# A hybrid SSM / short-convolution / expert-retrieval layer: reordering the stages ahead of the first expert gather

## The reference

```
sh1, sc1, g1, sh2, sc2, g2 = split(silu(cond) @ w_mod + b_mod)      # one row for context, one for latent
h = rmsnorm(x, norm1_g) * (1 + sc1) + sh1
u, cb, cc, ch = split(h @ w_in)
y_ssm  = glu(gelu(S5 scan of u, forward + backward, 32 groups x 64 complex states, + d_skip * u))
y_conv = cb * conv3(cc * ch)                                        # width 3 along rows
x = x + g1 * (concat(rmsnorm(y_ssm), headwise rmsnorm(y_conv)) * out_norm_g) @ w_out
h = rmsnorm(x, norm2_g) * (1 + sc2) + sh2
x = x + g2 * peer(h)
y = rmsnorm(x, final_norm_g)
```

## Time and profile before

| | |
|---|---|
| median of 3 runs | 1988.73 us |
| lowest, highest | 1987.07, 1994.5 us |
| the profiled execution | 1987.85 us, its span 1986.1 us |
| PE busy | 1201.5 us, 60% |
| DVE busy | 1443.9 us, 73% |
| ACT busy | 375.6 us, 19% |
| POOL busy | 736.0 us, 37% |
| DMA | 745.90 MB, mean 376 GB/s |
| first gather issued | 234.18 us |

### The profile page before, as it was taken

The page is one execution under the profiler, slowest core; times in us unless marked ns, Lnnn a source line. Parts: engine busy times, 40 slices in busy tenths (PEclk is TensorE's granted clock), DMA queues, the critical chain, the costliest instruction groups (busy, mean ns, idle before and its releaser), DMA issues.

```text
span 1986.1 us, 22255 instructions
## 1 busy us (share of the span) xinstructions
PE 1201.5 (60%) x7540; PEld 465.5 (23%) x7540; DVE 1443.9 (73%) x3889; ACT 375.6 (19%) x845; POOL 736.0 (37%) x673
## 2 busy tenths in 40 slices
PE   5988988888867666666544443364344454444444
PEld 2557733333322222222111000021000011111001
DVE  8778367877766776766788777777777767877675
ACT  4241342122222221111111110121011111211110
POOL 3100132333433333343443444444444444344442
PEclk8999989999968877777655555575555556555555
DMA  8556499999989999999999999999999999999996
GB/s 337 170 186 209 155 394 383 358 394 389 395 339 390 382 393 394 401 403 388 421 421 420 415 417 413 421 407 414 416 415 420 409 414 410 416 421 404 415 414 258
DMA packets 126098, 745.90 MB, mean 376 GB/s; under 512 B 12112, under 2 KB 34896, under 8 KB 40352
## 3 DMA queue, kind: packets, MB, share of 16 engines
q0 software_dynamic: 92160, 671.13, 82.8%
q1 hardware_dynamic: 33824, 73.35, 10.5%
HBM read 741.78 MB, written 2.65 MB: 375 GB/s over the span
## 4 chain that ended last, share of the span: by engine, by line
DMA 31%; PE 29%; DVE 26%; issue 10%; ACT 2%; POOL 0%; DVEq 0%; POOLq 0%; SPq 0%; ACTq 0%
DMA r<-table,gidx 30%; DVE r L1675 8%; PE bank L843 7%; PE bank L811 6%; PE bank L920 3%; PE bank L931 2%; DMA r<-w_query 1%; DVE wgt L1687 1%; PE bank L778 1%; DVE r L1643 1%; DVE i L1617 1%; PE bank L539 1%; PE bank L638 1%; DVE i L1623 1%; DVE r L1618 1%
## 5 line engine op out<-in xcount | busy, mean ns | idle before, releaser
L1875 POOL DMA_INDIRECT r<-table,gidx x640 | 708.9, 1108 | 1063.9 <-PE bank L843 902.6
L1675 DVE CUSTOM_DVE_ANT_0 r<-r 128x1024 f32<-128x1024 f32 x640 | 779.9, 1224 | 310.9 <-DMA r<-table,gidx 292.3
L843 PE MATMUL bank<-r,wgt 128*32 128x512 f32 x2560 | 536.6, 923 | 727.7 <-DVE wgt L1687 709.0
L843 PEld LDWEIGHTS bank<-r,wgt 128*32 128x32 f32 x2560 | 61.4, 130 | 1102.7 <-DVE wgt L1687 1032.2
L1223 ACT ACTIVATE r<-r 128x2 f32<-128x2 f32 x320 | 65.1, 203 | 1045.7 <-DVE r L1675 1042.8
L811 PE MATMUL bank<-hT_r,r 128*128 128x512 f32 x256 | 120.4, 625 | 0.9 <-ACT hT_r L1079 0.9
L1684 DVE TENSOR_TENSOR r<-r 128x2 f32<-128x2 f32 x320 | 50.2, 157 | 82.0 <-ACT r L1223 82.0
L1687 DVE TENSOR_TENSOR wgt<-fold,r 128x64 f32<-128x64 f32 x320 | 72.0, 225 | 11.1
L811 PEld LDWEIGHTS bank<-hT_r,r 128*128 128x128 f32 x256 | 50.3, 202 | 75.9 <-issue 75.9
L1223 ACT ACT_TABLE_LOAD x51 | 65.4, 1283 | 0.9
L920 PE MATMUL bank<-hT_r,r 128*128 128x512 f32 x128 | 62.9, 636 | 0.0
(11 more groups left out here) (362 smaller groups left out, 1472.6 us busy)
## 6 DMA issues: line engine op xcount, KB each, us to landing
r<-w_mod SPq DMA_DIRECT2D x24, 1024.0 KB, 7.8
r<-w_query SPq DMA_DIRECT2D x15, 1024.0 KB
r<-table,gidx POOLq DMA_INDIRECT x640, 11.6
r<-w_tiles SPq DMA_DIRECT2D x12, 512.0 KB, 8.1
x_r<-w_tiles SPq DMA_DIRECT2D x10, 512.0 KB, 4.9
hT_r<-xT SPq DMA_DIRECT2D x4, 640.0 KB, 6.3
r<-w_u SPq DMA_DIRECT2D x1, 2048.0 KB, 31.3
r<-w_o SPq DMA_DIRECT2D x1, 2048.0 KB, 10.5
```

The lines of the kernel that those rows point to most:

```text
L843: last = mm(bank[ACC[b % 2][h]][to:to + TG, :], wgt[:, g % 2, e, :], rows[:, k % SLOTS, D + h * 512:D + (h + 1) * 512], start=(G % HEADS = ...
L1675: V.tensor_tensor_reduce(rows[:, s, 0:D], rows[:, s, 0:D], h2r[tg], 1.0, 0.0, ALU.mult, ALU.add, hid[:, par, k:k + 1]).then_inc(dot_done, 1)
L1875: G_.indirect_dma_start(rows[:, k % SLOTS, :], None, table, bass.IndirectOffsetOnAxis(gidx[:, e, k:k + 1], 0)).then_inc(row_in[k % SLOTS], 16)
```

## The change

Five regions are edited.

1. **`bc` is loaded in two parts**: its B half at its old place (`ld_bc`), its C half behind `w_u` (`ld_cc`).
2. **Front.** DVE makes input block 0 straight behind `Bb`, then the reciprocal, four scalings, the gains, four scalings. PE turns tiles 0, 1 behind slab 5 and 2, 3 behind slab 6, ahead of `mod_turn(0)`; ACT takes them ahead of the modulation. Tiles 4 to 7 are turned after k = 1; there is no group after k = 4.
3. **`CP`.** DVE makes all eight blocks; POOL's block, its buffer `tp` and `p9_ready` go, and POOL's `Bd` waits for `cp_ready`, of which there is now one.
4. **SP and slabs.** `WTC` begins with buffers 4 and 5; the glu's weights are loaded when two context tiles are through (`zc_mm` 2), ahead of tiles 6 and 7; `w_query` then goes ahead of tiles 8, 9, and `w_o` ahead of tiles 10, 11. Slab 20 is summed between the halves of M, 21 behind them, 22 ahead of `Y` instead of behind `conv_ctx(0)`. `spread_heads` stands ahead of output tile 6 instead of tile 4 (the order of tiles is 0, 1, 2, 3, 6, 7, 4, 5).
5. **DVE behind the scans.** Convolution and gate product come first (the gate product ahead of the last tap), segment 2 in place of 3, 3 in place of 4, and 4 behind the second normalised half. `lag_blocks` comes after the third step of the context scan.

```diff
-            sp.dma_start(bcs, bc).then_inc(ld_bc, 16)
+            sp.dma_start(bcs[:, 0:2], bc[:, 0:2]).then_inc(ld_bc, 16)
             for n in range(8):
                 load_mod(n)
             sp.dma_start(wu, w_u).then_inc(ld_wu, 16)
+            sp.dma_start(bcs[:, 2:4], bc[:, 2:4]).then_inc(ld_cc, 16)
...
-        WTC = [0, 1, 2, 3, 4, 5, 0, 1, 2, 3, 0, 1]
+        WTC = [4, 5, 0, 1, 2, 3, 0, 1, 2, 3, 0, 1]
...
-                    sp.wait_ge(zc_mm, (1, 2, 3, 4, 7, 8)[q - 6])
+                    sp.wait_ge(zc_mm, q - 3)
...
-            for q in range(4):
+            for q in range(2, 6):
                 load_conv_ctx(q)
             sp.wait_ge(us_mm, 2)
-            for q in range(4, 6):
+            for q in range(2):
                 load_conv_ctx(q)
             for n in range(18, 24):
                 load_mod(n)
-            for q in range(6, 10):
+            sp.wait_ge(zc_mm, 2)
+            for j in range(2):
+                sp.dma_start(wt[:, j, :, :], w_tiles[NCONV + j]).then_inc(wtg_in, 16)
+            for q in range(6, 8):
                 load_conv_ctx(q)
             sp.wait_ge(m_mm, 2)
             sp.dma_start(wqa, w_query[:, :, 0:DQ]).then_inc(ld_wq0, 16)
-            sp.wait_ge(zc_mm, 6)
-            for j in range(2):
-                sp.dma_start(wt[:, j, :, :], w_tiles[NCONV + j]).then_inc(wtg_in, 16)
-            for q in range(10, 12):
+            for q in range(8, 10):
                 load_conv_ctx(q)
             sp.wait_ge(mod_mm, 24)
             sp.dma_start(woA, w_o[:, 0:4, :, :]).then_inc(ld_woa, 16)
+            for q in range(10, 12):
+                load_conv_ctx(q)
...
+            pe.wait_ge(silu_done, 1)
+            for n in range(KD):
+                mod_slab(n)
+                if n in (5, 6):
+                    turn_input(2 * (n - 5))
+                    turn_input(2 * (n - 5) + 1)
+            mod_turn(0)
...
-                if k in (1, 4):
-                    for e in range(4):
-                        turn_input((0 if k == 1 else 4) + e)
+                if k == 1:
+                    for e in range(4, 8):
+                        turn_input(e)
...
                 last.then_inc(m_mm, 1)
-            mod_slab(20)
-            mod_slab(21)
+                mod_slab(20 + a)
+            mod_slab(22)
...
-            mod_slab(22)
             mod_slab(23)
...
-                    if first and m == 4:
+                    if first and m == 6:
                         spread_heads()
...
+            for e in range(4):
+                take_input(e)
             mod_rows(0)
             mod_take(0)
...
             dve.wait_ge(bb_ready, 1)
             chunk_inputs(0)
-            gains(1, COL_N1, 2)
+            dve.wait_ge(rms_act, 2)
+            link(V.reciprocal(rs, rs))
+            for k in range(KD):
+                if k == 4:
+                    gains(1, COL_N1, 2)
+                tt(hT[:, k, :], hT[:, k, :], rs, ALU.mult).then_inc(xs_ready, 1)
             for n in range(1, 4):
                 chunk_inputs(n)
...
-            for q4 in range(CP_POOL, NQ, 4):
+            dve.wait_ge(ld_cc, 16)
+            for q4 in range(0, NQ, 4):
...
-                if i == 4:
+                if i == 3:
                     lag_blocks()
...
-            link(*[stt(cvx[:, i, 0:CTX - 1], ccx[:, i, 1:CTX], cw[2][i], cvx[:, i, 0:CTX - 1], ALU.mult, ALU.add) for i in range(KS)])
-
             dve.wait_ge(sgc_ev, KS)
             tt(mixc[:, 0:KS, :], mixc[:, 0:KS, :], gTc, ALU.mult).then_inc(gluc_ev, 1)
-            segment_products(3)
+            link(*[stt(cvx[:, i, 0:CTX - 1], ccx[:, i, 1:CTX], cw[2][i], cvx[:, i, 0:CTX - 1], ALU.mult, ALU.add) for i in range(KS)])
+            segment_products(2)
...
             pool.wait_ge(bb_ready, 1)
-            pool.wait_ge(xs_ready, KD)
+            pool.wait_ge(cp_ready, 1)
             link(G_.memset(Bd, 0.0))
```

More of the change, by code:

```diff
@@ L114, in build @@
         P9r = part(r2, 10816, 576).rearrange("p (j r q) -> p j r q", j=Q + 1, r=2)
-        tp = part(r2, 11392, 576).rearrange("p (q j c) -> p q j c", q=4, j=Q + 1)
         tv = part(r2, 11968, 576)
@@ L251, in build @@
         cp_ready = sem("cp_ready")
-        p9_ready = sem("p9_ready")
+        ld_cc = sem("ld_cc")
         bb_ready = sem("bb_ready")
@@ L367, in build @@
         HID_AT = {3: (0,), 4: (1,), 5: (2,), 6: (3,), 7: ()}
-        CP_POOL = 4
         CW = MCH * P
@@ L514, in _ @@
                 mm(bank[5][:, 0:CTX], ones[:, :], sq[k % 2][:, 0:CTX], start=(k == 0), stop=(k == KD - 1)).then_inc(sq_used, 1)
[L515 to L518, removed]
             def turn_input(e):
@@ L600, in _ @@
             pe.wait_ge(bd_ready, 1)
-            pe.wait_ge(cp_ready, 2)
+            pe.wait_ge(cp_ready, 1)
             pe.wait_ge(dm_ready, 1)
@@ L1108, in _ @@
                 modulate(0, k, 1, CTX, T).then_inc(h_ready, 1)
-            for e in range(8):
+            for e in range(4, 8):
                 take_input(e)
@@ L1132, in _ @@
             last.then_inc(dm_ready, 1)
-            act.wait_ge(cp_ready, 2)
+            act.wait_ge(cp_ready, 1)
             act.wait_ge(bp_ready, 2)
@@ L1426, in _ @@
             V.tensor_copy(sv[:, 9, :], sv[:, 4, :]).then_inc(bb_ready, 1)
-            dve.wait_ge(rms_act, 2)
-            link(V.reciprocal(rs, rs))
-            for k in range(KD):
-                tt(hT[:, k, :], hT[:, k, :], rs, ALU.mult).then_inc(xs_ready, 1)
             def chunk_inputs(n):
@@ L1559, in _ @@
             link(*[stt(cvx[:, i, 1:CTX], ccx[:, i, 0:CTX - 1], cw[0][i], cvx[:, i, 1:CTX], ALU.mult, ALU.add) for i in range(KS)])
-            link(*[stt(cvx[:, i, 0:CTX - 1], ccx[:, i, 1:CTX], cw[2][i], cvx[:, i, 0:CTX - 1], ALU.mult, ALU.add) for i in range(KS)])
             dve.wait_ge(sgc_ev, KS)
             tt(mixc[:, 0:KS, :], mixc[:, 0:KS, :], gTc, ALU.mult).then_inc(gluc_ev, 1)
-            segment_products(3)
+            link(*[stt(cvx[:, i, 0:CTX - 1], ccx[:, i, 1:CTX], cw[2][i], cvx[:, i, 0:CTX - 1], ALU.mult, ALU.add) for i in range(KS)])
+            segment_products(2)
             dve.wait_ge(rms_c, 1)
             V.reciprocal(inv1[0], rt1[0]).then_inc(inv_ready, 1)
-            segment_add(3)
+            segment_add(2)
             dve.wait_ge(inv_mm, 1)
@@ L1572, in _ @@
             last.then_inc(mixc_ready, 1)
-            segment_store(3)
+            segment_store(2)
             dve.wait_ge(zc_mm, 12)
             tt(mixc[:, KS:KD, :].rearrange("p k t -> p (k t)"), cvx.rearrange("p k t -> p (k t)"), bank[2][:, :], ALU.mult).then_inc(cvx_ev, 1)
-            segment_products(4)
+            segment_products(3)
             dve.wait_ge(rms_c, 2)
             V.reciprocal(inv8, rt8).then_inc(inv_ready, 1)
-            segment_add(4)
-            segment_store(4)
-            V.tensor_copy(small[:, 2:3], eps_c[:, :]).then_inc(scan_lat, 1)
+            segment_add(3)
+            segment_store(3)
             dve.wait_ge(inv_mm, 2)
@@ L1587, in _ @@
             last.then_inc(mixc_ready, 1)
+            segment_products(4)
+            segment_add(4)
+            segment_store(4)
+            V.tensor_copy(small[:, 2:3], eps_c[:, :]).then_inc(scan_lat, 1)
             dve.wait_ge(ld_xc, 16)
@@ L1846, in _ @@
             pool.sem_inc(bd_ready, 1)
-            pool.wait_ge(p9_ready, 1)
-            pool.wait_ge(ld_bc, 16)
-            for q4 in range(0, CP_POOL, 4):
-                q = slice(q4, q4 + 4)
-                w = P9 if q4 < NPAIR else P9r
-                J = Q + 1
-                pw = [w[:, :, r, q].rearrange("p s (q a) -> p q s a", a=1).broadcast_to([P, 4, J, GC]) for r in range(2)]
-                cv = [bcs[:, 2 + r, q, :].rearrange("p q (a c) -> p q a c", a=1).broadcast_to([P, 4, J, GC]) for r in range(2)]
-                o = [CP[:, r, q, :, :] for r in range(2)]
-                T_ = G_.tensor_tensor
-                link(T_(o[0], pw[0], cv[0], ALU.mult), T_(tp, pw[1], cv[1], ALU.mult))
-                link(T_(o[0], o[0], tp, ALU.subtract))
-                link(T_(o[1], pw[0], cv[1], ALU.mult), T_(tp, pw[1], cv[0], ALU.mult))
-                link(T_(o[1], o[1], tp, ALU.add))
-                link(G_.tensor_scalar(o[1], o[1], -1.0, None, ALU.mult))
-            pool.sem_inc(cp_ready, 1)
             pool.wait_ge(mod_tr, 6)
```

4 lines of the change are left out of this document (removed).

## The result

The changed kernel takes **1972.91 us** (median of 5 runs, 1966.37 to 1977.83); the kernel before, run beside it on the same chip, took 1988.73 (5 runs, 1987.07 to 1994.5). The ratio is 0.9911, 95% interval [0.9886, 0.9936], which is 17.7 us less (the two medians themselves lie 15.8 apart). The forecast was 1972 in a range of 1965 to 1980. The time was right; the sum behind it was not right in every term, and the places where it failed are the useful part of what follows.

The account below looks back on a forecast made before the run. Expert gathers (DMA) set the pace from 900 us; before the first gather at 234 us the chain, mostly PE, counts. Terms 4.1+2.3+3.2+5.5+1.6 = 16.7 off 1987.85 give 1971.2; plus 0.88 for the median, 1972 us, range 1965 to 1980.

Parts of the forecast that it names:

- What bounds the kernel: Up to the first gather at 234 us, each microsecond saved on the chain comes off the end; everything behind slides.
- Input blocks ahead of the scalings: In the modulation, gains end at 38.7 and PE starts at 40.1: 4.1 us earlier, bounds 2.2 and 5.2.
- sign of being wrong: In the front: PE's turns waiting for DVE's blocks would show the prediction wrong.
- rival B: Modulation becomes late: turns at half clock hold slab 7, second stall appears; gain 10.3 us, time 1978.4; chance 0.12.
- Turned tiles: The u stage loses one of its two groups of four turns: 2.3 us.
- CP: PE's wait ahead of the third group of state products goes whole: 3.2 us, with 4.8 us of cover left.
- The issue stall: PE's 3.13 us stall before 151.93, read as instruction fetch queued behind two slabs: 1.6 us saved, 4.4 better to 3.1 worse.
- rival D: First u matmuls run warm (2.6 us) and the stall goes whole (4.4 for 1.6): gain 22.1, 1966.6 us; chance 0.15.
- Rival A: The stall before 151.93 has another cause, queues being taken in turn, and stays: gain 15.1, 1973.6 us; chance 0.15.
- SP's order and slabs: Earlier glu weights and moved slabs let the glu run at once, ending at 177.7 instead of 183.28: 5.5 us.
- DVE's order: Behind the scans, DVE would wait for PE's glu, not PE for DVE, so the new order gains nothing.
- `lag_blocks` earlier: On DVE, moves up one step: under 1 us, and PE waits for the scan's end anyway: 0.

Follow-up runs that it names:

- front_only: Kernel before with only input block 0 ahead of the scalings, turned tiles between the slabs and CP wholly on DVE: 1979.26 us, ratio 0.9950 to before.
- slabs_back: Changed kernel with slabs 20 and 21 behind M, 22 and 23 behind the first convolution pass, as before: 1972.68 us, ratio 0.9927 to before.
- sp_order_back: Changed kernel with SP's old order of loads and old buffers, glu weights behind six convolution tiles: 1973.76 us, ratio 0.9924 to before.
- dve_order_back: Changed kernel with DVE's old order behind the scans, such as segment 2 ahead of the convolution: 1978.88 us, ratio 0.9941 to before.

## Why the prediction was right, and where it was not

**What bounds the kernel: right.** Three comparisons of the whole change give 0.9911, 0.9897 and 0.9897, that is 17.7 to 20.5 us off the end, and the first gather starts 20.4 us earlier (mean of three profiles after, 213.2, against the mean of two before, 233.6). What is saved ahead of the first gather reaches the end, and the rest slides. It did not stay "unchanged within 3 us" in a pair of profiles, because single executions differ by up to 12 us there.

**Input blocks ahead of the scalings: right**, 4.7 for 4.1, inside its bounds. The sequence was as worked out (block 7.0, gains at 37.7, floor `w_u`). I had the clock come back midway, and the nine profiles of this front differ there. In seven PE summed slab 5 at full clock (1.07 us), and the `u` stage began at 39.2 to 40.0. In three of the seven (`front_only`, `slabs_back`, `sp_order_back`) the first turns then waited 0.93 to 1.05 us for DVE's block and took 1.82 to 1.97, at half clock, and full clock was back by the second turns. That wait was a sign of being wrong in the prediction; the start at 39.6 to 39.8 shows no loss from it. In the other two slab 5 took 1.93 and the start came at 41.0 and 41.3: rival B's mechanism, in two executions of nine, at 1.5 to 2 us. What ends PE's wait ahead of the first `u` matmul is `w_u` in four of the nine (39.2 to 40.0) and ACT's modulated tile in the other five, so both bind at about the same time. The first eight `u` matmuls took 6.17, mostly at half clock, as taken (5.37 to 6.36 over the nine).

**Turned tiles: right**, 2.3. **CP: the wait went and the cover was 4.7, as said, but the term was mis-sized:** 4.4 for 3.2. I counted the wait of 3.17 and overlooked that the row behind it already shows 96 state products in 5.45, which at full clock take 4.15. Here the half clock behind the wait went with the wait.

**The issue stall: mechanism half right, size wrong.** The step that failed is "I take half of the stall for half of the bytes". All of it went, 4.5 us with the half clock behind it, which is the upper bound that the prediction gave and rival D's value. The backlog explains 2.5 us of it; 2.0 stay without it, and there PE still goes on only 2.5 us behind the instruction packet. So the rows point to the fetch of instructions, as the prediction read it, but it is late for more than the backlog. The Trainium skill, DMA: Bandwidth & Descriptors, section Queues, rings and completion order, has each DMA engine take its queues in turn, packet by packet. The traces agree in so far as the packet came at 149.5, 1.5 us before the slab data ended; but with slabs in flight it came 3.3 to 4.2 us into `Y` instead of 1.4, so taking turns did not spare it a delay. Rival A, that the stall stays in the changed kernel, is refuted.

**SP's order and slabs: right in size**, 5.6 for 5.5 up to the end of the glu.

**DVE's order: wrong reading.** The failed step is "DVE then waits for PE's glu, not PE for DVE. Segment 2 no longer stands ahead of the convolution ... Nothing". I compared DVE's time on the old scale (free at 171.45) with a PE that had moved by 1 us (174.0). But the edits ahead moved PE by 15.7 us and the latent scan, which DVE starts when the context scan is through, by only 10.9. On the new scale PE's input is there at 158.4 and DVE free at 160.5; DVE is the later one, and with the old order it would have been 5 us later still. `dve_order_back` puts 8.2 us on it. The forecast total survived because the order was in the change: I counted the SP term of 5.5 as if PE alone bounded the tail, and the DVE edit is what made that true. That was luck: nothing in the sum weighed it.

**`lag_blocks` earlier:** M started 11.9 us sooner, `Y` 11.2; worth nothing at `Y`, as said.

So the median of 1972.91 agrees with 1972 better than the terms do, and that closeness is luck too: the sum was some 4 us too small, and the later medians of the same kernel were 1969.84 and 1966.82.

## What to carry to other kernels

When several edits move two engines that meet further on, price every later step on the new scale of both: an order that costs nothing now can be the bound once its neighbour has moved, and putting it back is the experiment that shows it. A wait on PE can cost more than its length, since the matmuls behind it may run at half clock: 3.17 us of wait cost 4.4 here, while behind pauses of 2.43 and 2.59 the clock held. Read the row after the wait and add in what it lost. And before a difference between two profiles is explained, take a second profile of each: here the front repeated within 2 us and the gather part only within 12.

## What the hardware did that I had not expected

- An "issue" idle of PE can be moved and removed by the place of loads that have nothing to do with it: 2.88 to 3.81 us in the four profiles of kernels with two 1024 KB slabs issued together ahead of `Y`, 1.03 and 0.85 with none in flight, 0 to 0.5 with the slabs spread out. K, without a stall before, got one of 0.6 to 1.0 us in eight of the nine profiles with the new front. It ends 2.3 to 2.5 us behind a packet of the instruction queue in all eight, and the five profiles without it are those in which PE had waited 3.17 or 4.69 us at the state products, with that packet 1 to 2 us ahead of K instead of up to 0.4 into it. So it looks like the stall of `Y` again, a fetch that PE overtakes once it no longer waits; no run changed this by itself. In the changed kernel it stands on the chain, and DVE's `lag_blocks` wait 0.57 us for it.
- The same program began its `u` stage between 39.3 and 40.0 us in three profiles, and one edit away from it at 41.0 or 41.3, with PE at half clock in the slabs ahead after a pause of 2.6 to 2.8 us; in other executions it kept full clock after pauses of 2.4 and 2.6.
- A 1024 KB load of `w_query` beside the first gathers takes 25 to 27 us and stands on the chain in six of 13 profiles, of changed and unchanged kernels alike, and stays off it in the others. What decides it was not tried.
